# The first four groups of an input projection, with K outermost and beside conditioning in blocks of 512 columns

## What is computed

```python
mod = (silu(c) @ w_ada[l] + b_ada[l])              # 9 sequences x 6*2048
sh1, sc1, g1, sh2, sc2, g2 = split_cols(mod, [2048] * 6)
h = rms_norm(x, norm_mix[l]) * (1.0 + sc1) + sh1
y = mixer(h @ w_in[l]) @ w_out[l]
x = x + g1 * y
h = rms_norm(x, norm_mlp[l]) * (1.0 + sc2) + sh2
x = x + g2 * (relu(h @ w_up[l]) ** 2 @ w_down[l])
```

## Time and profile before

| | |
|---|---|
| median of 3 runs | 2745.33 us |
| the profiled execution's own time | 2747.8 us |
| its span | 2746.0 us, 54745 instructions |
| busy: TensorE / VectorE / ScalarE / POOL | 96% / 57% / 36% / 11% |
| granted TensorE clock, mean | 0.971 |
| read from HBM, written | 602.77 MB, 13.26 MB |

### The profile page before, as it was taken

The page is one execution under the profiler, slowest core; times in us unless marked ns, Lnnn a source line. Parts: engine busy times, 40 slices in busy tenths (PEclk is TensorE's granted clock), DMA queues, the critical chain, the costliest instruction groups (busy, mean ns, idle before and its releaser), DMA issues.

```text
span 2746.0 us, 54745 instructions
## 1 busy us (share of the span) xinstructions
PE 2623.0 (96%) x22336; PEld 2455.7 (89%) x22336; DVE 1567.1 (57%) x2327; ACT 981.7 (36%) x1081; POOL 315.0 (11%) x283
## 2 busy tenths in 40 slices
PE   6699989999999999999999999989999999999998
PEld 3289878989999999999999998988999999999998
DVE  2356445465445545545556888986665564554554
ACT  1133324333223233223344454445433333333333
POOL 1102042100000000000021334531100000000000
PEclk9599989999999999999999999999999999999999
DMA  9977877979999999999855454454555555555553
GB/s 326 346 232 235 272 237 245 297 253 299 296 294 297 297 296 300 302 296 293 256 184 168 139 162 155 139 167 141 154 183 176 176 183 175 177 183 176 176 183 108
DMA packets 589981, 616.17 MB, mean 224 GB/s; under 512 B 10431, under 2 KB 584093, under 8 KB 589313
## 3 DMA queue, kind: packets, MB, share of 16 engines
q1 hardware_dynamic: 583154, 591.70, 68.6%
q0 software_dynamic: 6720, 22.96, 2.6%
HBM read 602.77 MB, written 13.26 MB: 224 GB/s over the span
## 4 chain that ended last, share of the span: by engine, by line
PE 84%; DMA 6%; DVE 5%; issue 2%; ACT 1%; POOL 1%; SPq 0%; DVEq 0%; ACTq 0%; POOLq 0%
PE ps L793 25%; PE ps L794 24%; PE ps L795 24%; PE pm L851 5%; DMA araw_first<-in_w_ada 3%; DMA out_new_gla_sample<-st 1%; PE pm L866 1%; PE pm L963 1%; DVE w_lo L1731 1%; DMA out_new_hgrn_sample<-st 1%; DVE z L2192 1%; ACT w_hi L1312 1%; PE ps L851 1%; DVE acc L2192 1%; DMA raw<-in_ev_w_in 0%
## 5 line engine op out<-in xcount | busy, mean ns | idle before, releaser
L1731 DVE TENSOR_TENSOR w_lo<-raw,w_hi 128x1024 fp32r<-128x1024 f32 x705 | 883.1, 1254 | 967.0 <-ACT w_hi L1312 965.9
L1312 ACT ACTIVATE w_hi<-raw 128x1024 fp32r<-128x1024 f32 x736 | 778.3, 1059 | 1554.7 <-PE ps L795 1495.0
L793 PE MATMUL ps<-h_hi,w_hi 128*128 128x264 f32 x3840 | 1125.7, 293 | 18.9 <-DVE h_lo L1842 7.7
L794 PE MATMUL ps<-h_lo,w_hi 128*128 128x264 f32 x3840 | 1104.1, 288 | 0.0
L795 PE MATMUL ps<-h_hi,w_lo 128*128 128x264 f32 x3840 | 1103.0, 287 | 0.0
L793 PEld LDWEIGHTS ps<-h_hi,w_hi 128*128 128x128 f32 x3840 | 735.4, 191 | 53.4 <-issue 45.7
L794 PEld LDWEIGHTS ps<-h_lo,w_hi 128*128 128x128 f32 x3840 | 734.6, 191 | 0.6
L795 PEld LDWEIGHTS ps<-h_hi,w_lo 128*128 128x128 f32 x3840 | 734.2, 191 | 0.0
L793 PE MATMUL ps<-f_hi,w_hi 128*128 128x264 f32 x2048 | 587.5, 287 | 0.0
L794 PE MATMUL ps<-f_lo,w_hi 128*128 128x264 f32 x2048 | 583.7, 285 | 0.0
L795 PE MATMUL ps<-f_hi,w_lo 128*128 128x264 f32 x2048 | 583.0, 285 | 0.0
(11 more groups left out here) (305 smaller groups left out, 1458.2 us busy)
## 6 DMA issues: line engine op xcount, KB each, us to landing
araw<-in_w_ada SPq DMA_DIRECT2D x160, 1024.0 KB, 9.2
raw<-in_mlp_w_up SPq DMA_DIRECT2D x128, 1024.0 KB, 5.9
raw<-in_mlp_w_down SPq DMA_DIRECT2D x128, 1024.0 KB, 5.7
raw<-in_od_w_in SPq DMA_DIRECT2D x48, 1024.0 KB, 5.1
araw_first<-in_w_ada SPq DMA_DIRECT2D x32, 1024.0 KB, 10.0
raw<-in_ev_w_in SPq DMA_DIRECT2D x32, 1024.0 KB, 6.0
raw<-in_ev_w_out SPq DMA_DIRECT2D x16, 1024.0 KB, 5.8
raw<-in_od_w_out SPq DMA_DIRECT2D x16, 1024.0 KB, 5.7
```

Source lines behind the costliest of these rows:

```text
L793: nc.tensor.matmul(acc, w_hi[:, slot, cols], xh[:, k, :], start=(k == 0), stop=False)
L794: nc.tensor.matmul(acc, w_hi[:, slot, cols], xl[:, k, :], start=False, stop=False)
L1312: nc.scalar.activation(w_hi[:, u, :], raw[:, p, u, :], ACT.Copy).then_inc(hi_ready, 1)
L1731: nc.vector.tensor_tensor(w_lo[:, p, u, :], raw[:, p, u, :], w_hi[:, u, :].bitcast(F32), ALU.subtract).then_inc(lo_ready, 1)
```

## The change

- Shift and scale of layer 0's first norm come in eight blocks of 512 columns (`wide`), scale and shift of 512 features by turns, each as four loads of 1 MiB (4 K tiles x 512 columns) through four buffers: the place of `araw` and 16 tiles of `z`.
- x is loaded first. After the first block of each pair come 2 MiB of weights: four K tiles of the 1024 columns of groups 0 to 3, in two loads of 512 columns.
- h is made in four quarters of four K tiles, as soon as their scale and shift are there, by VectorE and ScalarE; POOL has no part in it.
- Groups 0 to 3 are multiplied a quarter at a time (`quarter_products(q, u)`: group u, K tiles 4q to 4q + 3). Between quarters VectorE takes the partial sums out and adds them up in `z`. Two blocks of conditioning stand between the products of each of the quarters 0 to 2. The gate products go by quarters too, gate-up stands in quarter 3.
- The loop of input groups runs from 4. The 16 conditioning groups beside it (the gate of the mixer's branch, then the scale of the second norm; now numbered from 0) stand two beside each of groups 4 to 7, one beside each of 8 to 15; SP's loads of them stand between the halves of the weights.
- `mixer0` loses its idle steps ahead of the recurrence, which starts in group 4 as before.
- `pool_w` and the two state copies move behind `level_shares(0)` on POOL's queue.

```diff
-ADA_IN0, ADA_OUT0, ADA_MLP0, ADA_ALL = 16, 32, 40, 96
+ADA_IN0, ADA_OUT0, ADA_MLP0, ADA_ALL = 0, 16, 24, 80
+WIDE = 512
+QUARTERS = D // WIDE
+WIDES = 2 * QUARTERS
+
+
+def ada_cols(a):
+
+
+    return a + (16 if a < ADA_IN0 + 8 else 24 if a < ADA_OUT0 else 8)
+
+
+def wide_at(w):
+
+
+    return QUARTERS * (w // 2) + (SH1 if w % 2 else SC1)
...
-        araw_first = at("araw_first", [P, 4, KT // 2, GC], F32, o_h)
...
+        wides = [at(f"wide{i}", [P, 4, WIDE], F32, o) for i, o in
+                 enumerate((o_araw, o_araw + 8192, o_z + 16 * T * 4, o_z + 16 * T * 4 + 8192))]
+        x_rows = at("x_rows", [P, NCH, D], F32, o_h)
...
+        def half_rows(t, p, h):
+            return t[:, p, 2 * h:2 * h + 2, :].rearrange("p u (k n) -> p (u k) n", n=WIDE)
+        def quarter_unit(t, p, u):
+            return half_rows(t, p, u // 2)[:, :, (u % 2) * GC:(u % 2 + 1) * GC]
...
-            for a in range(ADA_IN0):
+            x_in()
+            w = kview(io["ev_w_in"][0])
+
+            def wide(b):
+
+                for c in range(4):
+                    i = 4 * b + c
+                    if i >= 4:
+                        sp.wait_ge(wide_used, i - 3)
+                    sp.dma_start(wides[i % 4][:, :, :], ada[0][:, 4 * c:4 * c + 4, wide_at(b) * P:wide_at(b) * P + WIDE]
+                                 ).then_inc(wide_in[i % 4], 16)
+
+            for q in range(QUARTERS):
+                wide(2 * q)
                 for h in range(2):
-                    i = 2 * a + h
-                    if i >= 4:
-                        sp.wait_ge(ada_used, i - 3)
-                    sp.dma_start(araw_first[:, i % 4, :, :],
-                                 ada[0][:, 8 * h:8 * h + 8, a * GC:(a + 1) * GC]).then_inc(ada_first_in[i % 4], 16)
-                if a == 1:
-                    x_in()
-
-            def of0(a0):
-                return a0, lambda i: (ada[0], (a0 + i) * GC)
-
-            w = kview(io["ev_w_in"][0])
-            phase(8, 0, w, lambda i: i * GC, rates=of0(ADA_IN0))
-            def scales0(a0):
-                return a0, lambda i: (ada[0], (a0 + i + 8) * GC)
-
-            phase(4, 8, w, lambda i: (12 + i) * GC + 16, rates=scales0(ADA_IN0 + 8))
-            phase(4, 12, w, lambda i: (8 + i) * GC, rates=scales0(ADA_IN0 + 12))
+                    if q >= 2:
+                        sp.wait_ge(split_used, NU * (q - 2) + (2 * h + 2))
+                    sp.dma_start(half_rows(raw, q % 2, h), w[:, UK * q:UK * q + UK, h * WIDE:(h + 1) * WIDE]
+                                 ).then_inc(raw_in[q % 2][h], 16)
+                wide(2 * q + 1)
+
+            def rates0(a):
+                ada_group(a, ada[0], ada_cols(a) * GC)
+
+            for i in range(4, 16):
+                col = i * GC if i < 8 else i * GC + 4 * GC + 16 if i < 12 else i * GC - 4 * GC
+                half(i, i % 2, w, col, 0, 0)
+                if 6 <= i <= 8:
+                    rates0(2 * i - 10)
+                elif i > 8:
+                    rates0(i - 1)
+                half(i, i % 2, w, col, 0, 1)
+                if i <= 8:
+                    rates0(i - 4 if i < 6 else 2 * i - 9)
             w = kview(io["ev_w_out"][0])
...
@@ pool @@
-            pool.wait_ge(tr_ready, START_BANKS)
...
+            for _ in level_shares(0):
+                pass
+            pool.dma_start(pool_w[:, :, :, :], io["ev_pool_w"][0].rearrange("g (c p) e -> p g c e", p=P)).then_inc(aw_in, 16)
...
@@ tensor @@
+            def wide_half(w, half):
+
+                if w and half == 0:
+                    pe.wait_ge(wide_rows, w)
+                for c in (2 * half, 2 * half + 1):
+                    i = 4 * w + c
+                    pe.wait_ge(wide_in[i % 4], 16 * (i // 4 + 1))
+                    for q in range(4):
+                        last = nc.tensor.matmul(pm[q * CP:(q + 1) * CP, 3, :], c_pad[:, 4 * c + q, :], wides[i % 4][:, q, :],
+                                                start=(c == 0), stop=(c == 3), tile_position=(0, q * CP))
+                    last.then_inc(wide_used, 1)
+
+            def wide_turn(w):
+
+                pe.wait_ge(wide_rows, w + 1)
+                if w:
+                    pe.wait_ge(wide_ready, w)
+                for m in range(QUARTERS):
+                    last = turn(pm[:, 2, m * P:(m + 1) * P], mod_rows[:, m * P:(m + 1) * P], P)
+                last.then_inc(wide_turned, 1)
...
+            def quarter_products(q, u):
+
+
+                n = NU * q + u
+                if n >= 2:
+                    if n - 2 < 3 * NU:
+                        pe.wait_ge(part_taken, n - 1)
+                    else:
+                        pe.wait_ge(evacuated, n - 3 * NU - 1)
+                pe.wait_ge(lo_ready, n + 1)
+                low = quarter_unit(w_lo, q % 2, u)
+                for kk in range(UK):
+                    k = UK * q + kk
+                    if u == 0:
+                        pe.wait_ge(h_ready, k + 1)
+                    for m in range(MT):
+                        acc = ps[:, MT * (u % 2) + m, 0:T]
+                        cols = slice(kk * GC + m * P, kk * GC + (m + 1) * P)
+                        nc.tensor.matmul(acc, w_hi[:, u, cols], h_hi[:, k, :], start=(kk == 0), stop=False)
+                        nc.tensor.matmul(acc, w_hi[:, u, cols], h_lo[:, k, :], start=False, stop=False)
+                        last = nc.tensor.matmul(acc, low[:, kk, m * P:(m + 1) * P], h_hi[:, k, :], start=False, stop=(kk == UK - 1))
+                last.then_inc(split_used, 1)
+
+            def gate_rows(q):
+
+
+                if q == 0:
+                    pe.wait_ge(aw_lo, 1)
+                    pe.wait_ge(rstd_ready, 1)
+                for k in range(UK * q, UK * q + UK):
+                    cols = slice(16 * k, 16 * k + P)
+                    nc.tensor.matmul(pm[:, 0, 0:T], a_hi[:, cols], h_hi[:, k, :], start=(k == 0), stop=False)
+                    nc.tensor.matmul(pm[:, 0, 0:T], a_hi[:, cols], h_lo[:, k, :], start=False, stop=False)
+                    last = nc.tensor.matmul(pm[:, 0, 0:T], a_lo[:, cols], h_hi[:, k, :], start=False, stop=(k == KT - 1))
+                return last
+
+            for w in range(2):
+                wide_half(w, 0)
+                wide_half(w, 1)
+                wide_turn(w)
+            for q in range(QUARTERS - 1):
+                for u in range(NU):
+                    w = 2 * q + 2 + u // 2
+                    wide_half(w, u % 2)
+                    quarter_products(q, u)
+                    if u % 2:
+                        wide_turn(w)
+                gate_rows(q)
+            quarter_products(3, 0)
+            gate_rows(3).then_inc(alr_psum, 1)
+            quarter_products(3, 1)
+            pe.wait_ge(alr_ready, 1)
+            for h in range(3):
+                last = nc.tensor.matmul(pm[:, (1, 2, 0)[h], 0:T], gate_up[:, h * DK:(h + 1) * DK], a_lr[:, :], start=True, stop=True)
+            last.then_inc(gate_psum, 1)
+            quarter_products(3, 2)
+            pe.wait_ge(gz_ready, 1)
+            nc.tensor.matmul(pm[:, 1, 0:T], gate_up[:, 3 * DK:4 * DK], a_lr[:, :], start=True, stop=True).then_inc(gate_psum, 1)
+            quarter_products(3, 3)
 
...
-            for i in range(16):
+            for i in range(4, 16):
+                first, second = (2 * i - 8, 2 * i - 7) if i < 8 else (None, i)
+
                 def beside(u):
+                    if u == 0 and first is not None:
+                        ada_turn(first)
                     if u == 1:
+                        ada_group(second)
+                    if u == 2:
+                        ada_turn(second)
+                    next(mixer, None)
...
+                if first is not None:
+                    ada_group(first)
...
@@ scalar @@
+            for q in range(QUARTERS):
+                for u in range(NU):
+                    hi_quarter(q, u)
+                shift_quarter(q)
...
@@ vector @@
+            def wide_copy(w):
+
+                dve.wait_ge(wide_used, 4 * w + 4)
+                if w:
+                    dve.wait_ge(wide_turned, w)
+                nc.vector.tensor_copy(mod_rows[:, :], pm[:, 3, :]).then_inc(wide_rows, 1)
+
+            def wide_add(w):
+
+                c = wide_at(w)
+                dve.wait_ge(wide_turned, w + 1)
+                parts = pm[:, 2, :].rearrange("p (m q n) -> p m n q", m=QUARTERS, n=CP)[:, :, 0:NC, :]
+                nc.vector.tensor_reduce(mod_sum[:, :, :], parts, AX.X, ALU.add).then_inc(wide_summed, 1)
+                dve.wait_ge(wide_summed, w + 1)
+                nc.vector.tensor_tensor(modf[:, c:c + QUARTERS, :], mod_sum[:, :, :],
+                                        badaf[:, c:c + QUARTERS].unsqueeze(2).broadcast_to([P, QUARTERS, NC]),
+                                        ALU.add).then_inc(wide_ready, 1)
...
+            def shift_quarter(q):
+
+                tiles, sh = slice(UK * q, UK * q + UK), SH1 + UK * q
```

(34 more changed lines are left out.)

381 lines of the change are left out of this document (166 added, 215 removed).

## The result

The changed kernel takes **2728.06 us** (median of 4 runs, 2721.83 to 2730.50); the kernel before, run beside it, 2746.22. The ratio is 0.9934, 95% interval 0.9912 to 0.9955: faster, by 18 us. The profiled execution took 2728.19 us, span 2726.4, against 2747.8 and 2746.0 before, so the traces differ by 19.6. Forecast were 2708 us and 40.1. The sign was right; half of the gain is missing.

A forecast was written before the change was run, and what follows sets the result against it. TensorE was taken as busy nearly the whole span, with loads setting the pace at the start. Terms -53.2 + 9.5 + 3.6 = -40.1 us took 2747.8 to 2707.7, forecast 2708; range 2694 to 2727.

The forecast's parts named there:

- step 6: POOL's moved transfers, and the untouched work from group 8 on: no change in either, with bounds for POOL's part.
- same instructions, nothing: Groups 8 to 15, layer 0's output, both MLPs and layer 1: unchanged instructions, so no time gained or lost.
- step 1: Loads at the start: 2 KB rows move at 385 GB/s, 2.72 us per MiB, where 1 KB rows took 3.01.
- Packets gain nothing: Rival on the start's loads: longer rows bring no rate, 9.5 us later, 2717 us; chance 0.25.
- step 2: Start: x there at about 10 us, TensorE at the first wide at 31, next load landing at 37.2.
- steps 3 and 4: Quarters and their tail: loads set the pace, last piece at 127.0, group 4 begins at 149.9 us: -53.2 us.
- TensorE stays at half clock through the quarters: Rival: a quarter takes 42.0 us, group 4 no earlier, 2762 us; chance 0.05, two slow quarters 0.05.
- step 5: Groups 4 to 7: +9.5 us for one conditioning group more in each, +3.6 for late loads.
- by my working its first level is ready 4 us ahead of its turn, so nothing: Recurrence from group 4: losing its idle steps ahead costs no time.
- Nothing, with bounds of -5 and +8: POOL's three DMAs and two copies, moved behind the level work: 0 us, bounds -5 and +8.
- supply or the recurrence's lost slack: Rival: groups 4 to 7 lose 3 us each, not 0.9, the states 8: 2724 us; chance 0.20.

The follow-up runs named there:

- e2: Changed kernel with each 1 MiB load of a wide issued as two transfers of 256 columns, so rows of 1 KB instead of 2 KB: 2734.82 us.
- e5: Changed kernel with 24 matmuls whose result nobody reads ahead of the third half of a wide in each quarter: 2728.65 us.
- c2: Changed kernel with six edits: wait on summed, wide 0 between x's transposes, earlier POOL transfers, early row copy, folded column offset, 24 unread matmuls: 2704.66 us.
- e4: Changed kernel with VectorE copying conditioning group 0's rows ahead of the decay's logarithm steps instead of behind them: 2722.37 us.
- e3: Changed kernel with the second load of conditioning queued ahead of the second half of the weights for groups 5 to 8: 2729.24 us.
- e9: Changed kernel loading only one k tile of eight for conditioning groups 1, 3, 5 and 7, whose modulation is thus not computed: 2730.03 us.
- e7: Changed kernel with the pooling weights and two state copies issued when the wides are all used, instead of at group 4's shares: 2722.52 us.
- c1: Changed kernel with four edits: wait on summed instead of mod_ready, wide 0's matmuls between x's transposes, earlier POOL transfers, early copy of conditioning rows: 2707.18 us.
- e1: Changed kernel with the addition's column offset 16 folded into the base of its two tiles, leaving the loop's value to register arithmetic: 2724.05 us.

## Why the prediction was half right

The step that failed is the last sentence of step 6, "same instructions, nothing": 9.2 of the 20.5 missing us are lost there. The other terms fell short by less: 4.6 ahead of group 4, 3.9 in groups 4 to 7, 2.8 in group 8.

**Price of a load (step 1): right.** 385 GB/s forecast, 387 measured, and about 350 for 1 KB rows (e2). "Packets gain nothing" is refuted. The Trainium skill, DMA: Bandwidth & Descriptors, section Specifications, gives a core about 358 GB/s of HBM; the measurement decides against it for a core that runs alone.

**Start (step 2): 1.7 late.** x landed at 11.35, not 10; TensorE came to the first wide at 32.67, not 31; wide 1's first piece was there at 38.90, not 37.2.

**Stream and tail (steps 3 and 4): right but for the clock.** 90.85 us from 38.90 to the last piece at 129.75 (e5), forecast 89.8; from there to group 4 22.95 (e5) and 22.94 (c2), forecast 22.9. The kernel after adds 1.9 by products at the slow rate, since it begins the last piece at 131.6 instead of 129.75. 1.7 + 1.05 + 1.9 is the 4.6. "TensorE stays at half clock through the quarters" did not come: it was 0.66 to 0.78 in four stretches of ten us and 1.00 from 80 to 120. The Trainium skill, TensorE: Matmul & The Clock Gate, section HAM oscillation, describes a kernel whose work per K tile is shorter than its wait for the next load and which falls back to the slow clock at every K tile. This trace agrees only in part: the clock fell at some of the waits and came back between them, and it cost 1.9 us, not 54.

**Groups 4 to 7 (step 5): 17.0 instead of 13.1.** The term "by my working its first level is ready 4 us ahead of its turn, so nothing" failed in its reason: TensorE waits 2.08 us for `mod_rows` at 161.67, and e4 shows that the copy stood behind the recurrence's logarithm steps. But e4 shows it to be worth nothing by itself. Of the 6.6 us of waits for conditioning 4.2 stand in these groups, priced at 3.6; the other 2.4 are group 8's. From copy to copy groups 5 to 7 took 22.3, 21.2 and 23.2 us, where 20 to 21 were forecast. Neither e3 nor e9 shortened the waits, so where the 3.9 us go is open beyond these two rows.

**POOL (step 6): a wrong term of 2.8 us.** "Nothing, with bounds of -5 and +8" was read from a mean over a stretch with a DMA share of 0.79; the place where the transfers went has 0.98, and a load that TensorE waits for was issued right behind them:

```profile
220.00:243.00 23.00, 21.07 (x205) 18.29 (x204) 12.96 (x20) 7.33 (x9) 5.27 (x6) 1.00 0.98 313
```

Measured with e7: 2.8 us in group 8, and the same in c1 and c2. The bound held it, the value taken did not.

**"Groups 8 to 15, layer 0's output, both MLPs and layer 1: same instructions, nothing": the wrong term.** 9.2 us were lost in the loops, 28.7 to 19.5. 4.7 of them are the wait: the instructions of TensorE are the same, but VectorE's register steps for one address are not, and they put the addition 0.10 or 0.19 us later, at a wait that had no slack. That is 0.09 us in each of 55 groups. 2.8 are 0.05 us a group inside the products, with no cause shown. 1.7 are the first group at a lower granted clock, which traces with the same code have or have not. No step looked at what a renumbering (`a_at` from 0 to 16) makes an engine's queue compute, nor at how near to its edge the wait stood. That the new number is what brought the second register step is argued from the program: the fold (e1) left two steps, and no run gives the groups their old numbers.

The rival "supply or the recurrence's lost slack", 2724, came nearest in time, and for the wrong reason: it had 8.4 more in groups 4 to 7 and 8 at the states; measured were 3.9 in groups 4 to 7 and 2.8 in group 8, by POOL's transfers, and the rest at places it did not name. That it came near is luck. The range, 2694 to 2727, gave the untouched 2280 us no error at all.
